# Routing the first expert tile beside the output projection, and spreading the gate projection over four column strips

## The reference, cut to what matters

```python
def _hybrid_mixer(...):                       # once per layer
    px, pc = ux @ w_in, uc @ w_in             # includes 16 gate columns per row
    gates = g + b_gate                        # log input and forget gates, 8 rows each
    ...                                       # mLSTM and neighbourhood attention
    return jnp.concatenate([ml, na], -1) @ w_out

def _peer(u, wq, sub_keys, up, down):         # blocks of 128 rows
    q = (ub @ wq).reshape(tb, 8, 2, 128)
    s1, s2 = einsum(q[:, :, 0], sub_keys[:, 0]), einsum(q[:, :, 1], sub_keys[:, 1])
    # top 16 of each half, top 16 of the 256 sums -> 16 experts per row and head
    g = softmax(top)
    act = gelu(einsum('td,tkd->tk', ub, up[eidx]))
    return einsum('tk,tkd->td', g * act, down[eidx])

x = LN(alpha * x + g1 * mixer(...));  x = LN(alpha * x + g2 * _peer(x * (1 + sc2) + sh2))
```

## Time and profile before

| what | us |
|---|---|
| median of 3 runs (4603.65 to 4612.15) | 4607.52 |
| the profiled execution | 4609.56 |
| its span | 4607.8 |
| PE busy | 3903.4 (85%) |
| DVE busy | 3237.5 (70%) |
| POOL busy | 1524.9 (33%) |
| ACT busy | 796.7 (17%) |

### The profile page before, as it was taken

How to read it: one execution, slowest core, us unless ns; L and a number is a source line. 1 busy time by engine, 2 the same in 40 slices (tenths; PEclk the granted TensorE clock), 3 DMA queues, 4 the chain that set the end, 5 groups by cost and what they waited for, 6 DMA issues and landing times.

```text
span 4607.8 us, 46202 instructions
## 1 busy us (share of the span) xinstructions
PE 3903.4 (85%) x11216; PEld 1862.7 (40%) x11216; DVE 3237.5 (70%) x8467; ACT 796.7 (17%) x2152; POOL 1524.9 (33%) x1425
## 2 busy tenths in 40 slices
PE   8998897888888888888888879989788888888887
PEld 3435754333333333333333334466433333333332
DVE  3106746888888888888888743075688888888885
ACT  1002321111111111111111111133111111111111
POOL 1100102444444444444444410000244444444442
PEclk9998899999999999999999999979999999999999
DMA  7632125999999999999999951122599999999998
GB/s 270 215 112 62 65 96 223 427 421 413 414 422 402 424 427 398 423 419 385 427 408 408 427 211 55 53 74 101 213 421 427 405 416 427 390 421 427 402 427 343
DMA packets 243743, 1486.01 MB, mean 323 GB/s; under 512 B 25120, under 2 KB 49952, under 8 KB 72848
## 3 DMA queue, kind: packets, MB, share of 16 engines
q0 software_dynamic: 191232, 1385.58, 72.7%
q1 hardware_dynamic: 52368, 98.79, 6.5%
HBM read 1477.87 MB, written 2.21 MB: 321 GB/s over the span
## 4 chain that ended last, share of the span: by engine, by line
PE 38%; DMA 29%; DVE 15%; issue 13%; POOL 2%; ACT 1%; DVEq 1%; POOLq 0%; SPq 0%; ACTq 0%; PEldq 0%
DMA arena<-in_updown,arena 28%; PE ps L786 12%; PE ps L778 5%; PE ps L623 4%; PE ps L638 3%; PE ps L747 3%; POOL arena L1084 2%; DVE arena L1441 2%; DVE arena L1450 2%; PE ps L643 2%; PE ps L716 2%; PE ps L672 1%; PE ps L618 1%; PE ps L705 1%; PE ps L574 1%
## 5 line engine op out<-in xcount | busy, mean ns | idle before, releaser
L786 PE MATMUL ps<-arena 128*128 128x512 f32 x5120 | 2419.6, 611 | 534.2 <-DVE arena L1441 529.1
L1084 POOL DMA_INDIRECT arena<-in_updown,arena x1280 | 1444.5, 1128 | 2099.3 <-PE ps L786 1610.6
L1450 DVE CUSTOM_DVE_ANT_0 arena<-arena 128x1024 bf16<-128x1024 f32 x1280 | 1566.4, 1224 | 289.5 <-DMA arena<-in_updown,arena 247.3
L786 PEld LDWEIGHTS ps<-arena 128*128 128x128 f32 x5120 | 919.7, 191 | 1982.8 <-DVE arena L1441 1138.3
L999 ACT ACTIVATE arena<-arena 128x1 f32<-128x1 f32 x1280 | 259.2, 203 | 2669.7 <-DVE arena L1450 2649.2
L1441 DVE TENSOR_SCALAR arena<-CN,arena 128x128 f32<-128x128 f32 x1280 | 444.0, 347 | 224.2 <-PE ps L786 196.8
L778 PE MATMUL ps<-arena 128*128 (+1 forms) x1280 | 297.8, 387 | 18.5 <-DVE arena L1382 16.1
L778 PEld LDWEIGHTS ps<-arena 128*128 128x128 f32 x1280 | 249.2, 195 | 87.7 <-issue 36.2
L1071 POOL TENSOR_TENSOR arena<-arena 128x256 f32<-128x256 f32 x64 | 40.4, 663 | 662.3 <-DMA arena<-in_bias 662.3
L623 PE MATMUL ps<-arena 128*128 128x512 f32 (+1 forms) x672 | 236.7, 509 | 0.0
L623 PEld LDWEIGHTS ps<-arena 128*128 128x128 f32 x672 | 126.8, 192 | 114.0 <-issue 103.1
(11 more groups left out here) (195 smaller groups left out, 2777.5 us busy)
## 6 DMA issues: line engine op xcount, KB each, us to landing
arena<-in_ada_w POOLq DMA_DIRECT2D x40, 1024.0 KB, 5.3
arena<-in_updown,arena POOLq DMA_INDIRECT x1280
arena<-in_wq SPq DMA_DIRECT2D x32, 512.0 KB, 4.2
arena<-in_w_in SPq DMA_DIRECT2D x6, 2048.0 KB, 10.4
arena<-in_w_in SPq DMA_DIRECT2D x24, 512.0 KB, 3.9
arena<-in_ada_w SPq DMA_DIRECT2D x4, 2048.0 KB, 14.3
arena<-in_bias SPq DMA_DIRECT2D x16, 512.0 KB, 4.0
arena<-in_w_out SPq DMA_DIRECT2D x2, 4096.0 KB, 12.9
```

The costliest lines, as they stand in the source:

```text
L786: mm = e.matmul(ps[hf][:], diag[:, k % 2, :], ring[:, k % RING, D + hf * 512:D + (hf + 1) * 512], start=False, stop=False, skip_group_chec ...
L1084: e.indirect_dma_start(ring[:, k % RING, :], None, updown, bass.IndirectOffsetOnAxis(ap=idx16[:, k:k + 1], axis=0)).then_inc(sem(f"rows{k ...
L1450: e.tensor_tensor_reduce(prod[:, k % 2, :], ring[:, k % RING, 0:D], u, 1.0, 0.0, ALU.mult, ALU.add, dots[:, k:k + 1]).then_inc(sem("L.dot_ ...
```

## The change

- **Gates.** Each G matmul is split over four column strips. Strip s takes a quarter of the rows as its moving side and writes PSUM partitions 32s to 32s + 7. So there are four times as many matmuls and ACT copies, each a quarter as wide, and three more small loads of the bias.
- **Barrier.** The barrier between output projection and experts is gone. PE runs the projection in halves (`out_half`). After the fourth half come `turn_u(0)`, then the folds of heads 0 to 2 and the scores of heads 0 and 1 between the later halves. DVE interleaves `residual_norm` with the first modulation and the two routings. The score of head 2 waits until DVE has read the last tile.
- **Key fold.** The folds of heads 3 to 7 move into units 0 to 4 of the first tile: a quarter of a head before each of k = 1, 3, 5, 7, copied out by ACT after k = 3, 5, 7, 9. In these units the key scores move from k = 8 to k = 11. `wqT` is loaded straight to where the folded result will stand, a head (1 MB) at a time, with no wait. Folds use two banks instead of four.
- **Memory.** The eight ring slots are laid over the projection's weights (4), its input `mixT` (3) and the rows of the residual (1). POOL starts gathers 0 to 6 once the last `y_ready` has come, and gather 7 after `ln1_done`. `keys` lies over `ln2r`, `g1r` over `last_slot`, and so `g2r` is loaded after `ln1_done` and `ln2r` after the last fold.

```diff
@@ input projection, PE and ACT @@
-                            mm = e.matmul(bank[0:8, 0:width], wgs[:, k, 8 * i:8 * i + 8], uT[:, k, cols], start=(k == 0), stop=(k == KD - 1))
+                            for s in range(4):
+                                mm = e.matmul(bank[32 * s:32 * s + 8, 0:piece], wgs[:, k, 8 * i:8 * i + 8],
+                                              uT[:, k, cols.start + s * piece:cols.start + (s + 1) * piece], start=(k == 0), stop=(k == KD - 1))
...
+                        for s in range(4):
+                            ins = e.activation((li, lf)[i][:, tc.start + s * piece:tc.start + (s + 1) * piece], bank[32 * s:32 * s + 8, 0:piece], ACT.Identity, bias=bgs[32 * s:32 * s + 8, i:i + 1])
@@ PE, projection and first scores @@
-                meet(e, "pe")
...
+                def fold(h, q):
+
+                    n, c, j = 4 * h + q, 2 * h + q // 2, q % 2
...
+                    if n >= 2:
+                        e.wait_ge(sem("L.wk_evac"), n - 1)
+                    for k in range(4):
+                        mm = e.matmul(ps[6 + n % 2][:, k * P:(k + 1) * P], wk[:, c, 4 * j + k, :], keys[:, c, :], start=True, stop=True)
+                    mm.then_inc(sem("L.wk_mm"), 1)
...
+                def first_scores(h):
+
+                    e.wait_ge(sem("L.uT_ready"), 1)
+                    e.wait_ge(sem("L.wk_evac"), 4 * (h + 1))
+                    if h == LEAD:
+                        e.wait_ge(sem("L.y_read"), nt)
+                    key_scores(h, h, ps[4 + h] if h < LEAD else ps[2], None)
+
+                for x in range(2 * nt):
+                    out_half(x // 2, x % 2)
+                    if x == 3:
+                        turn_u(0)
+                    if 4 <= x < 4 + LEAD + 1:
+                        for q in range(4):
+                            fold(x - 4, q)
+                    if 5 <= x < 5 + LEAD:
+                        first_scores(x - 5)
+                first_scores(LEAD)
...
+                def folding_unit(h):
+
+                    for k in range(TOPK):
+                        if k in FOLD_AT:
+                            fold(h + LEAD + 1, FOLD_AT.index(k))
+                        if k == LATE_KEY_AT:
+                            e.wait_ge(sem("L.wk_evac"), 4 * (h + LEAD + 2))
+                            key_scores(h + LEAD + 1, h + LEAD + 1, ps[2], h + LEAD + 2)
+                        weigh(h * TOPK, k)
@@ ACT @@
+                root_first(0)
+                root_first(1)
                 e.wait_ge(sem("L.uT_mm"), 1)
...
+                for h in range(LEAD + 1):
+                    for q in range(4):
+                        fold_out(h, q)
+                    if h == 0:
+                        root_first(2)
                 for h in range(LEAD):
                     gate_exp(h, PH - LEAD + h)
+                for m in range(3, nt):
+                    root_first(m)
@@ POOL @@
+                    if k == 0:
+                        e.wait_ge(sem("L.y_ready"), nt)
+                    if k == RING - 1:
+                        e.wait_ge(sem("L.ln1_done"), 1)
@@ DVE @@
+                    residual_norm(0)
                     e.wait_ge(sem("L.u_rows_loaded"), 32)
...
+                    residual_norm(1)
+                    residual_norm(2)
                     for h in range(LEAD):
...
-                        for _ in route(h, PH - LEAD + h, 2 + h % 2):
+                        for _ in route(h, PH - LEAD + h, 4 + h):
...
+                    residual_norm(3)
                     for h in range(LEAD):
                         gate_norm(h, PH - LEAD + h)
-                    e.wait_ge(sem("L.row2_loaded"), 32)
+                    for m in range(4, nt):
+                        residual_norm(m)
+                    e.sem_inc(sem("L.ln1_done"), 1)
```

More of the change, by code:

```diff
@@ L384, in build @@
         gate_all = r(PH * TOPK)
-        ysb = r(D)
         gsum = r(PH)
@@ L409, in build @@
         sd = r(2)
+        u = r(D)
+        r = Region(residual_at)
+        last_slot = r(2 * D)
+        g2r = r(D)
+        junk = r(D)
+        ysb = r(D)
+        prod = junk.bitcast(BF16).rearrange("p (a d) -> p a d", a=2)
+        WO_SLOTS, MIX_SLOTS = KD * D // (2 * D), KD * T // (2 * D)
+        ring = [Region(wo_at + n * 2 * D)(2 * D) for n in range(WO_SLOTS)] + [Region(mixer_top + n * 2 * D)(2 * D) for n in range(MIX_SLOTS)] + [last_slot]
+        assert len(ring) == RING
         ps = [ctx.enter_context(nc.psum_tensor(f"ps{i}", [P, 512], F32)) for i in range(8)]
@@ L762, in _, with out_half @@
-                meet(e, "pe")
-                nt = NT - t0
+                nt = NT - t0
+                def out_half(m, hf):
+                    if m == 0 and hf == 0:
+                        e.wait_ge(sem("L.wo_loaded"), 16)
+                    if m >= 2 and hf == 0:
+                        e.wait_ge(sem("L.y_read"), m - 1)
+                    for k in range(KD):
+                        mm = e.matmul(ps[2 * (m % 2) + hf][:], mixT[:, k, (t0 + m) * P:(t0 + m + 1) * P], wo[:, k, hf * 512:(hf + 1) * 512],
+                                      start=(k == 0), stop=(k == KD - 1))
+                    if hf == 1:
+                        mm.then_inc(sem("L.y_ready"), 1)
@@ L796, in unit, with tile @@
                         weigh(un * TOPK, k)
-                def tile(t, more):
+                def folding_unit(h):
[6 more added lines that the diff above has]
+                        weigh(h * TOPK, k)
+                def tile(t, more, first=False):
                     e.wait_ge(sem("L.acc_free"), t + 1)
                     for hf in range(2):
-                        e.matmul(ps[hf][:], zero, ln2r[:, 0, 0:512], start=True, stop=False, skip_group_check=True)
+                        e.matmul(ps[hf][:], zero, CN[:, 0:512], start=True, stop=False, skip_group_check=True)
+                    if first:
+                        for h in range(3):
+                            folding_unit(h)
+                        turn_u(t + 1)
+                        for h in range(3, PH - LEAD - 1):
+                            folding_unit(h)
+                        e.wait_ge(sem("L.uT_ready"), t + 2)
+                        e.sem_inc(sem("pe_token"), 1)
+                        with e.Fori(PH - LEAD - 1, PH) as h:
+                            unit(t, h, h + (LEAD + 1 - PH))
+                        close(t)
+                        return
                     with e.Fori(0, 3) as h:
@@ L999, in unit @@
                         e.activation(acts[:, k:k + 1], dots[:, k:k + 1], ACT.Gelu_apprx_tanh).then_inc(sem("L.act_done"), 1)
+                        if folded is not None and k in FOLD_EVAC_AT:
+                            fold_out(folded, FOLD_EVAC_AT.index(k))
                         if k == EXP_AT and route:
@@ L1005, in tile @@
                 def tile(t, more, first):
-                    unit(t, 0, True, None if first else t - 1)
-                    with e.Fori(1, PH - LEAD - 1) as h:
-                        unit(t, h, True)
+                    if first:
+                        for h in range(PH - LEAD - 1):
+                            unit(t, h, True, None, h + LEAD + 1)
+                    else:
+                        unit(t, 0, True, t - 1)
+                        with e.Fori(1, PH - LEAD - 1) as h:
+                            unit(t, h, True)
                     if more:
@@ L1337, in _, with residual_norm @@
                 meet(e, "dve")
-                e.wait_ge(sem("L.row1_loaded"), 48 if q_ctx else 32)
-                for t in range(t0, NT):
-                    m = t - t0
+                def residual_norm(m):
+                    t = t0 + m
                     w = tmp[:, m % 2, :]
+                    if m == 0:
+                        e.wait_ge(sem("L.row1_loaded"), 32)
+                    if q_ctx and t == NCT:
+                        e.wait_ge(sem("L.g1_lat_loaded"), 16)
                     e.wait_ge(sem("L.y_ready"), m + 1)
```

151 lines of the change are left out of this document (69 added, 82 removed).

## The result

The changed kernel takes 4564.42 us (median of 4 runs, 4561.09 to 4565.21) against 4605.73 for the kernel before (median of 4 runs, 4603.65 to 4612.15). The ratio is 0.9905, interval 0.9893 to 0.9917. It is faster and inside the range of 4509 to 4568, but by 41 us and not by the 77 that 4530 stood for. The profiled execution took 4563.95, its span 4562.1, 45.7 less than the span before.

What follows compares the result with a forecast made beforehand. The prediction took the expert stage to be bound by its gathers on full DMA engines. Terms 70.7 - 8 - 4 + 20 = 78.7 us off the profiled 4609.6 gave 4530.9, 4528.8 for the median, stated as 4530; range 4509 to 4568.

Steps and rivals of the forecast that it cites:

- The start of the gathers: Projection start to gather 0: 106.6 us instead of 142.2 in layer 0, 79.1 instead of 114.2 in layer 1.
- the one stall of 3.3 us: In the projection, PE waits some 3.3 us after the second quarter fold, because ACT takes `root_first(2)` before copying fold 1.
- DVE's margin: In layer 0's projection, `y_read` of tile 3 comes at 82.5, PE needs it at about 92: 9 us to spare.
- The start carries through: Ninth gather goes at 123 and 99.4 us, before eight are through; DMA stays fed, the whole start is kept: +70.7 us.
- 1.049 / 426 = 2.46 us: Expert stage: time of one gather, 128 rows of 8 KB (1.049 MB) at 426 GB/s; 16 gathers make a 39.4 us unit.
- Loads among the gathers: `g2r` and `ln2r` (1.57 MB) now load beside the gathers: up to 4.4 us per layer, 8.8 in all; 8 taken.
- Folding in the first tile: Ten folding units, mainly the late key score: 0.4 us per unit, 4 us in all; bounds 0 and 2 per unit.
- The rival in which these units become PE's: Each of ten folding units takes 2 to 4 us longer as PE work does not fit between gathers; 4556, chance 0.09.
- the one in which the fold serializes the loop: In folding units ACT, DVE and PE wait on each other: 11.1 us per unit, 111 in ten; 4637, chance 0.04.
- Gates: Four-strip gate matmuls gain 20 us, bounds -16 and 28: 11.4 in layer 1, only 8.5 counted in layer 0.
- the side-by-side reading of the four-strip row: L574 shows eight rows in 0.99 us, so strips run side by side, instructions at most 0.043 us apart.
- The estimate from the Trainium skill's 81 ns per matmul: Rule against the gates' gain: 256 rows x 0.081 = 20.7 us per layer, so no gain.

Runs made afterwards that it cites:

- the last experiment: The aligned kernel with gather 0, not only gather 7, waiting for DVE's last normalization (`ln1_done`): 4550.70 us, ratio 0.9869.
- The aligned kernel: The changed kernel with pads of 64, -64 and 96 bytes, so all eight ring slots start at a multiple of 256 bytes: 4530.78 us, ratio 0.9827.
- the reordered weights: The aligned kernel with modulation slices starting at job 20 instead of 17 and the first `wtok` load behind three `wch`: 4524.37 us, ratio 0.9817.
- the kernel without the row loads: The aligned kernel with the loads of `g2r` and `ln2r` cut to eight columns: 4527.58 us, ratio 0.9817.
- the kernel with 256 bytes of pad: The kernel before the change with only its ring moved 256 bytes later: 4608.28 us, ratio 0.9999.

## Why the prediction was right in one half and wrong in the other

- **The start of the gathers** was right: 107.4 and 79.6 us for 106.6 and 79.1, with the one stall of 3.3 us at its place. DVE's margin held; PE didn't wait for DVE before the last product. But the stall was priced too low: with the slower rows behind it, it cost 5.1 us in layer 0. The sum was 0.8 off and not 1.7 or more because its other terms were a little high.
- **The start carries through** was right too: the ninth gather at 123.8 for 123, and in the last experiment 16.4 of 19.1 us of delay went through the first tiles.
- **Where it failed** is the step that carries "1.049 / 426 = 2.46 us" for a gather over from the kernel before, and with it "the whole start is kept: +70.7 us". The change lays the ring slots over other memory, and the prediction gave that no line. The later tiles had no term, because nothing in their code changed. After the change a gather took 2.49 us. The runs put a term of -33 us there: -24.5 in the later tiles and -8.4 in the first tiles, for slots that don't start on a multiple of 256 bytes. With it the sum would have been 4530 + 33 = 4563; 4564.42 was measured. That this fits so well is partly luck: the gates gave 5.4 us less than counted, and loads, folds and late scores cost 6.2 less. The aligned kernel is what the prediction described: 81.0 us under the kernel before, for 77 forecast, with the same offsetting errors. The changed kernel stayed inside the range only because the high end, 4568, was set for rivals, and none of these came true.
- **Loads among the gathers**: 8 counted, 4.0 measured (1.5 and 2.5). The DMA engines' whole time (up to 4.4 per layer) was too much, and nothing was too little.
- **Folding in the first tile**: the 4 us were counted for the late key score. The folds and their copies measured 0. The late score has no run of its own; with the loads away, the first tiles are 2.0 and -0.2 us longer than before, and that bounds it. The rival in which these units become PE's falls, and the one in which the fold serializes the loop with it. PE is busy 36.9 of 40 us there and still not the bound. The lower bound of the term, 0, was close.
- **First tiles**: 12 predicted and 14.2 measured look like a hit, but the causes differ: 8.4 of alignment, 4.0 of loads, and 1.8 that stay open (about as much as such a stretch scatters).
- **Gates**: the side-by-side reading of the four-strip row was right; the 256 rows took 9.5 us in layer 1 (6 to 11 predicted) and the stage gained 10.6 for 11.4. In layer 0 the gain was 4.0 for 8.5. I had taken off some 3 us for the DMA; the waits behind the gates were 6.0 us (3.52 and 2.49), and the M group took 10.13 us at the lower clock where it took 7.13 with the reordered weights. The 4.0 isn't exact. Five kernels with the gates as before are the same up to the projection of layer 0, and it starts between 601.3 and 607.4 us, 604.7 on average; with the strips, in the changed kernel and four aligned ones with the old order of loads, it starts between 599.1 and 601.9, 600.1 on average, a gain of 4.6. The estimate from the Trainium skill's 81 ns per matmul ("TensorE: Matmul & The Clock Gate", Back-to-back issue gap), 20.7 us, falls. It took each of the 256 rows for a matmul; by 128 matmuls of two rows each it would be an estimated 10.4. The strips' rows came 22 ns apart and their matmuls 44, so 81 ns is too much either way. That strips run side by side stands; in the Trainium skill it is told in Part 3 of that page, under The mechanism and Measured speedup vs the span model, with some 4 ns between starts, and not in the list that the prediction names. The measured 22 ns are more than that.

**Open**: in layer 0, tile 1 of the kernel without the row loads is still 2.0 us longer than before (333.1 for 331.1), in layer 1 it isn't; the kernel with 256 bytes of pad, which should equal the one before, has 332.3 there, so it may be scatter or the late key score. And what PE waits for in the gaps of 1.7 to 2.8 us within the strips' rows, no view shows. No run was made for either. How the 256-byte boundary costs what it does inside a DMA engine isn't shown either.

## What to carry to other kernels

When a transfer that bounds a stage gets another place in memory, work out the start address of each slot and compare it with the old one, to the byte: the change of place is an edit of every transfer, also in the loops whose code is untouched. Here the pads that put the slots back on multiples of 256 bytes gave 33 us to a change that had gained 41 without them. Ask of a change not only which instructions it moves but which quantities (GB/s at full DMA share, here) it assumes unchanged, and give each a line in the sum, with a bound. A short idle of PE should be priced with the slower matmuls behind it, and PE work under a full DMA queue, like the folds here, at nothing as its lower bound.

## What the runs showed of the hardware

- Gathers of 8192-byte rows move 420 to 422 GB/s into slots that start 96 or 128 bytes (in the changed kernel 96 and 192) past a multiple of 256 bytes, and 426 to 427 into slots on such a multiple, at the same DMA share of 1.01. Ten tiles of such gathers take 1.0% longer. A start 256 bytes further is as good as one on a multiple of 1024.
- Four column strips of 32 let fp32 matmuls with 8 weight columns and 128 moving ones start 0.022 us apart (128 rows in 2.83 us), where one strip with 512 columns took 0.325 us a row (64 in 20.80).
- After a wait of 3.33 us the 16 rows behind it took 3.67 us, where the 16 before it took 1.95; the granted clock was 0.57.
- The 256 rows of the strips have one gap of 1.7 to 2.8 us in which the profile shows nothing that PE waits for (1.73 and 2.53 us in the changed kernel, 2.75 with the reordered weights).
